# Hybrid decoder layer on one core: two k-steps of the output projection as three fp32r terms

## The chip, the core and the metric

The kernel runs on one core of a Trainium2 chip. A core has TensorE (matmuls into PSUM), VectorE, ScalarE and GpSimd, each of which works through its own instructions in order, and DMA queues, of which this kernel uses that of SyncE (SP) for nearly everything. The engines meet through semaphores. The metric is the time of one execution on the device in microseconds (us). Lower is better. Three runs of the kernel before gave a median of 588.15 us (587.84 to 588.36).

## What is computed

One decoder layer on 256 tokens of width 1024, in fp32. The part that the change touches:

```python
def hybrid_mixer(x, mem, ...):
    h = rms_norm(x, norm_mix_g)
    q_sb, k_sb, v_sb, x_rg, gate_rg, q_ca = jnp.split(h @ w_in, IN_SPLITS, axis=-1)
    o_sb = merge_heads(stick_breaking_attention(...))                 # 512 columns
    hr = rg_lru(causal_depthwise_conv(x_rg, conv_w, conv_b), ...)
    o_rg = gelu(gate_rg) * hr                                         # 256 columns
    o_ca = memory_cross_attention(...)                                # 256 columns
    y = concatenate([rms_norm(o_sb, g_out_sb), rms_norm(o_rg, g_out_rg), rms_norm(o_ca, g_out_ca)])
    return y @ w_out

x = x + hybrid_mixer(...)
x = x + moe_ffn(rms_norm(x, norm_ffn_g), ...)    # 64 experts, 8 for each token, and a shared one
```

## The kernel before

**Stages.** The input projection and the three head groups take the first 84 us. Then comes the output projection, mixed with the end of cross-attention, up to 123 us. Then the router picks the experts and VectorE writes their order to `ids` (at about 137 us). The rest is the experts: TensorE gathers each group's tokens, multiplies, and scatters. The expert weights (3 MB each) stream through cells of 8 KB for each partition, in an order fixed in the code. Six experts are fixed and need no router; their loads and the shared expert's go out before the router is done. A load into a cell waits until TensorE is done with what the cell held.

**Output projection.** y has eight k-steps of 128 columns. Steps 0 to 3 are attention (group 0), 4 and 5 recurrent (group 1), 6 and 7 cross-attention (group 2). Each group is normalised with its own root, so its product is kept apart: `project(u)` (L1612) makes the product of one group, one tile of 128 tokens and one half of 512 columns in PSUM, and VectorE's `residual(u)` (L1153) multiplies it by the group's 1/rms and adds it to x1. There are twelve: the four of group 0, then group 1 and group 2 for tile 0, then for tile 1 in the order group 1, group 2 for each half. The fifth and sixth are thus recurrent, and so are the ninth and the eleventh. A matmul in fp32 leaves two records in the trace, one in fp32r leaves one.

**The sums.** The mean of squares of a group goes ScalarE (`square_and_gain`, L775: the square into `y_sq`, then the gain into `yT`), GpSimd (adds the k-steps, L678 to L684), TensorE (a sum over the partitions, units 26, 33 and 34, L1547), VectorE (`mean_square`, L1148), ScalarE (a root, L850), VectorE (the reciprocal in `residual`). Unit 34 is cross-attention's, and stands in TensorE's program behind the sixth projection and ahead of the seventh.

**What sets the order.** All of it is written out by hand: each engine's program is a list, up to unit 21 by `walk` (L368), after it by the calls in the text. VectorE's program around the change is: gelu's argument, four maxima of cross-attention (`ca_max`), norms, the recurrent scan, the recurrent rows (`yT`, L1188), `ca_evac` 2 and 3 (L1142), `ca_result(0)`, residuals 0 to 2, `ca_result(1)`, residual 3, `mean_square(1)`, residual 4, `mean_square(2)`, residuals 5 to 7, the mean of x1's squares for tile 0, residual 8 and so on. After residual 9 comes `low_part(0)` (L1226) and then residual 10.

**Three terms.** Elsewhere the kernel makes fp32 products from fp32r ones: ScalarE rounds a to a_hi, VectorE makes a_lo = a - a_hi, and TensorE adds a_hi*b_hi + a_lo*b_hi + a_hi*b_lo (L1487, L1509, L1520).

## Time and profile before

| | before |
|---|---|
| median of 3 runs | 588.15 us |
| profiled execution | 588.95 us |
| its span, first to last instruction | 587.2 us |
| TensorE busy | 552.8 us (94%) |
| VectorE busy | 208.9 us (36%) |
| ScalarE busy | 159.2 us (27%) |
| GpSimd busy | 24.3 us (4%) |
| read from HBM | 225.9 MB, 386 GB/s over the span |
| granted clock of TensorE, mean | 0.982 |
| output projection (L1624) on TensorE | 64 records, 29.4 us busy |

The profiled execution is one execution. Its own time is 1.75 us above its span and 0.8 us above the median. Busy times are of an engine's own instructions; a wait shows as idle time ahead of an instruction, with the instruction that ended it. Records of one engine overlap a little, so the distance between starts tells what an instruction costs in a row of its like.

### The profile page before, as it was taken

To read this page: it belongs to the slowest core of one execution; us is meant where nothing else is said; L and a number is where in the kernel's file an instruction comes from. 1 tells how busy PE (TensorE), PEld (TensorE's weight loads), DVE (VectorE), ACT (ScalarE), POOL (GpSimd) and SP (SyncE) were. 2 spreads that over 40 slices of the span, in tenths; PEclk is the share of its full clock that TensorE was granted. 3 is DMA by queue.
4 is the path that set the end of the run, shared out by engine and by line. 5 is a ranking of instruction groups with operands and counts; after the bars stand their busy time and mean duration, and the time that the engine had idled before them with its cause. 6 is when DMAs were issued, how large, how long until landed. Compare 5 with 4: busy or idle time off the path is not lost.

```text
span 587.2 us, 8291 instructions
## 1 busy us (share of the span) xinstructions
PE 552.8 (94%) x3148; PEld 305.7 (52%) x3149; DVE 208.9 (36%) x532; ACT 159.2 (27%) x307; POOL 24.3 (4%) x78
## 2 busy tenths in 40 slices
PE   8999999999999999999999999999969999289994
PEld 6988875465544445555344554555534455034441
DVE  2879789664335222220122222222221222102212
ACT  5786376242212112220021222222221211101112
POOL 1005240000000000000000000000000000000000
PEclk9999999999999999999999999999998999679999
DMA  8997559659999999999999999999999999999993
GB/s 318 418 419 289 214 204 424 253 222 350 424 395 419 423 421 420 427 427 423 426 423 426 426 419 430 431 423 423 424 429 426 431 420 436 428 411 410 417 408 142
DMA packets 26776, 227.50 MB, mean 387 GB/s; under 512 B 3184, under 2 KB 3312, under 8 KB 7664
## 3 DMA queue, kind: packets, MB, share of 16 engines
q1 hardware_dynamic: 26592, 226.93, 93.2%
q8 instruction: 26, 0.43, 0.3%
q14 instruction: 14, 0.11, 0.0%
q10 hardware_dynamic: 144, 0.03, 0.0%
HBM read 225.90 MB, written 1.05 MB: 386 GB/s over the span
## 4 chain that ended last, share of the span: by engine, by line
PE 79%; DMA 14%; DVE 4%; issue 1%; ACT 1%; SPq 0%; DVEq 0%; ACTq 0%
PE ps L1760 30%; PE ps L1789 13%; DMA cell_three<-in_w_e 9%; PE ps L1719 8%; PE ps L1799 7%; DMA cell_two<-in_w_e 5%; PE ps L1624 5%; PE ps L1520 4%; PE ps L1487 3%; PE ps L1501 2%; PE ps L1780 1%; PE ps L1509 1%; DMA wA<-in_w_qk 1%; PE ps L1766 1%; PE ps L1772 1%
## 5 line engine op out<-in xcount | busy, mean ns | idle before, releaser
L1760 PE MATMUL ps<-cell_two,xg 128*64 128x512 f32 (+2 forms) x496 | 110.0, 612 | 18.6 <-DMA cell_three<-in_w_e 14.0
L1789 PE MATMUL ps<-cell_d,e_hT 128*64 128x512 f32 (+2 forms) x440 | 87.6, 597 | 2.2 <-DVE e_hT L1383 1.5
L1760 PE MATMUL ps<-cell_gu,xg 128*64 128x512 f32 (+2 forms) x416 | 78.3, 594 | 0.0
L1380 DVE TENSOR_TENSOR e_h<-e_sg,ps 128x256 f32<-128x256 f32 x28 | 11.8, 421 | 186.2 <-ACT e_sg L897 186.2
L1760 PEld LDWEIGHTS ps<-cell_two,xg 128*64 128x64 f32 (+2 forms) x496 | 34.5, 132 | 82.6 <-issue 82.6
L897 ACT ACTIVATE e_sg<-ps 128x256 f32<-128x256 f32 x28 | 10.8, 384 | 208.5 <-PE ps L1760 208.5
L1438 DVE SCALAR_TENSOR_TENSOR ylo<-ps,gslot,yhi 128x512 fp32r<-128x512 f32 x52 | 39.0, 750 | 72.0 <-ACT yhi L908 72.0
L1719 PE MATMUL ps<-pick,xhi 128*128 128x256 f32 x224 | 58.5, 300 | 0.3 <-DVE pick L1296 0.3
L908 ACT ACTIVATE yhi<-ps,gslot 128x512 fp32r<-128x512 f32 x52 | 35.7, 687 | 69.4 <-PE ps L1789 69.3
L1719 PE MATMUL ps<-pick,xlo 128*128 128x256 f32 x224 | 54.3, 281 | 0.0
L1719 PEld LDWEIGHTS ps<-pick,xhi 128*128 128x128 f32 x224 | 42.2, 188 | 19.1 <-issue 18.8
L1760 PEld LDWEIGHTS ps<-cell_gu,xg 128*64 128x64 f32 (+2 forms) x416 | 25.6, 128 | 47.9 <-issue 47.6
L1789 PEld LDWEIGHTS ps<-cell_d,e_hT 128*64 128x64 f32 (+2 forms) x440 | 25.7, 126 | 40.0 <-issue 39.5
L1799 PE MATMUL ps<-yhi,S 128*128 128x512 f32 x104 | 43.0, 413 | 0.9 <-DVE ylo L1438 0.9
L1719 PEld LDWEIGHTS ps<-pick,xlo 128*128 128x128 f32 x224 | 42.4, 189 | 1.0 <-issue 1.0
L1799 PE MATMUL ps<-ylo,S 128*128 128x512 f32 x104 | 40.9, 393 | 0.0
L1760 PE MATMUL ps<-cell_three,xg 128*64 128x512 f32 (+1 forms) x144 | 37.9, 653 | 0.4 <-DMA cell_three<-in_w_e 0.4
L884 ACT ACTIVATE xg<-ps,vec 128x256 f32<-128x256 f32 x60 | 25.2, 472 | 23.7 <-PE ps L1719 23.6
L1624 PE MATMUL ps<-wo,yT 128*128 128x512 f32 x64 | 29.4, 601 | 0.4 <-DVE x L1163 0.4
L1422 DVE TENSOR_TENSOR xg<-ps,vec 128x512 f32<-128x512 f32 x26 | 18.0, 691 | 30.9 <-PE ps L1719 30.9
L904 ACT CAST S<-ps 128x256 fp32r<-128x256 f32 x26 | 9.7, 372 | 59.7 <-PE ps L1774 59.7
L1377 DVE TENSOR_REDUCE gslot<-ps 64x1 f32<-64x2 f32 (+2 forms) x64 | 10.0, 157 | 42.6 <-ACT S L904 41.4
(336 smaller groups left out, 674.7 us busy)
## 6 DMA issues: line engine op xcount, KB each, us to landing
cell_two<-in_w_e SPq DMA_DIRECT2D x31, 2048.0 KB, 25.8
cell_d<-in_w_e SPq DMA_DIRECT2D x51, 1024.0 KB, 22.1
cell_gu<-in_w_e SPq DMA_DIRECT2D x48, 1024.0 KB, 15.0
cell_three<-in_w_e SPq DMA_DIRECT2D x9, 3072.0 KB, 23.0
wo<-in_w_out SPq DMA_DIRECT2D x1, 4096.0 KB, 12.3
wA<-in_w_qk SPq DMA_DIRECT2D x7, 512.0 KB, 10.8
wR<-in_w_rest SPq DMA_DIRECT2D x3, 1024.0 KB, 28.6
wV<-in_w_v SPq DMA_DIRECT2D x1, 2048.0 KB, 18.8
```

The lines of the kernel that those rows point to most:

```text
L884: nc.scalar.mul(rows_of(c, slice(k, k + 1), slice(0, 2)).squeeze(1), ps[:, Y[step % 2], k % 2 * 2 * P:(k % 2 + 1) * 2 * P].rearrange("p (g ...
L908: nc.scalar.mul(yhi[:, half * 512:(half + 1) * 512], ps[:, Y[half], :], gslot[:, g.routed % 2:g.routed % 2 + 1]).then_inc(yhi_act, 1)
L1380: nc.vector.tensor_tensor(dst[:].rearrange("q k p -> q (k p)"), e_sg[:], ps[:, U, DE:2 * DE], ALU.mult).then_inc(sem, 1)
L1422: nc.vector.tensor_tensor(rows_of(g.chunk + 1, slice(2 * step, 2 * step + 2), slice(0, 2)), ps[:, Y[1], :].rearrange("p (k g s) -> p k g s ...
L1438: nc.vector.scalar_tensor_tensor(ylo[:, c], ps[:, Y[half], :], gslot[:, g.routed % 2:g.routed % 2 + 1], yhi[:, c].bitcast(F32), ALU.mult, ...
L1487: last = mm(b[:, 0:SEQ], part[:, k, :], a[:, k, :], start=k == 0 and m == 0, stop=k == KD - 1 and m == 2)
L1520: last = mm(b, a[:, k, c:c + P], w[:, k, :], start=k == 0 and m == 0, stop=k == KD - 1 and m == 2)
L1624: last = mm(ps[:, ACC[2 * t + half], :], yT[:, k, t * P:(t + 1) * P], wo[:, k, half * 512:(half + 1) * 512], start=k == chunks[0], stop=k ...
L1719: last = mm(o, part[:, t, k, :], pick[c % 2][:, t, :], start=i == 0, stop=i == 3)
L1760: last = mm(ps[side * w:(side + 1) * w, U, :], rows(k, slice(side * w, (side + 1) * w)), weight[:, k - k0, :], start=k == 0, stop=k == KD - 1)
L1789: last = mm(ps[side * w:(side + 1) * w, Y[half], :], e_hT[:, kk, side * w:(side + 1) * w], n[:, kk, half * 512:(half + 1) * 512], start=kk ...
L1799: last = mm(ps[:, ACC[2 * t + half], :], to_token[:, t * P:(t + 1) * P], y[:, half * 512:(half + 1) * 512], start=False, stop=sem is not N ...
```

## The change

w_out's k-steps 4 and 5 and the recurrent rows get high and low parts in fp32r. ScalarE makes `wo_hi` in `walk` (two casts of 128x1024, `split_o`), and the gained high rows `y_hi` (the two gains first, then the two squares; the gain is no longer written to `yT`). VectorE makes `wo_lo` ahead of its first maximum (`weight_low`) and `y_lo` behind `ca_evac(2)` and `ca_evac(3)` (`gain_low`). TensorE's fp32 products of steps 4 and 5 become three fp32r ones each. The parts lie where cells lie: `wo_hi` in that of low 5, so this load now waits until the eleventh projection is done, `wo_lo` in w_out's own place. `x1_sq` moves, so that down 6 need not wait for it. The loads around it are in another order.

```diff
--- before.py
+++ after.py
@@ -183,6 +183,10 @@
     wA = [at(f"wA{n}", o_A + 4 * KB * n, [P, KD, P]) for n in range(8)]
     wA_lo = [at(f"wA_lo{n}", o_A + 4 * KB * n, [P, KD, P], F32R) for n in range(8)]
     wo = at("wo", o_A, [P, KD, D])
+    wo_hi = at("wo_hi", o_ring + 80 * KB, [P, 2, D], F32R)
+    wo_lo = at("wo_lo", o_A + 16 * KB, [P, 2, D], F32R)
+    y_hi = at("y_hi", o_O + 16 * KB + 64, [P, 2, SEQ], F32R)
+    y_lo = at("y_lo", o_O + 12 * KB, [P, 2, SEQ], F32R)
     res = at("res", o_A, [P, NT, D])
     xg = at("xg", o_A, [P, KD // 2, 2, 2, P])
 
@@ -202,7 +206,7 @@
     rg_t = r("rg_t", [P, 2, SEQ])
     rg_u = r("rg_u", [P, 2, SEQ])
     y_sq = at("y_sq", o_R + 16 * KB, [P, KD, SEQ])
-    x1_sq = at("x1_sq", o_R + 8 * KB, [P, D])
+    x1_sq = at("x1_sq", o_A, [P, D])
     xhi = at("xhi", o_R, [P, NT, KD, P], F32R)
     xn2T = at("xn2T", o_R + 16 * KB, [P, KD, SEQ])
     yhi = at("yhi", o_R + 16 * KB, [P, D], F32R)
@@ -370,7 +374,7 @@
             if 3 <= i <= 10:
                 walk.append(("t", i - 3))
             walk += {1: [("split_w", 2)], 2: [("split_w", 3)], 3: [("split_u", 14)], 4: [("split_u", 15), ("split_u", 16)],
-                     5: [("split_u", 17)], 6: [("ca_square", 0)], 7: [("conv", 0)], 8: [("ca_norm", 0)], 9: [("conv", 1)],
+                     5: [("split_u", 17)], 6: [("ca_square", 0)], 7: [("conv", 0)], 8: [("ca_norm", 0)], 9: [("split_o", 0), ("split_o", 1), ("conv", 1)],
                      12: [("gelu", 0)]}.get(i, [])
 
 
@@ -536,16 +540,18 @@
             load_fixed("high", 4)
             load_fixed("down", 3)
             load_fixed("down", 4)
-            load_fixed("low", 5)
             load_fixed("low", 6)
+            sp.wait_ge(wo_ps, 4)
+            load_shared("low")
+            sp.wait_ge(yrg_dve, 2)
+            load_fixed("down", 6)
             sp.wait_ge(unit_ps, 33)
             load_fixed("high", 5)
+            sp.wait_ge(wo_ps, projections.index((1, 1, 1)) + 1)
+            load_fixed("high", 6)
+            load_fixed("low", 5)
             sp.wait_ge(wo_ps, len(projections))
-            load_fixed("high", 6)
             load_fixed("down", 5)
-            load_shared("low")
-            sp.wait_ge(ssq_act, 7)
-            load_fixed("down", 6)
             sp.wait_ge(rt_ps, NT)
             load_fixed("down", 2)
 
@@ -809,6 +815,9 @@
                 elif kind == "ca_norm":
                     act.wait_ge(ca_ss_dve, 1)
                     nc.scalar.activation(ca_rs[:], ca_rs[:], ACT.Sqrt).then_inc(ca_rt_act, 1)
+                elif kind == "split_o":
+                    act.wait_ge(wo_loaded, 16)
+                    nc.scalar.copy(wo_hi[:, n, :], wo[:, 4 + n, :]).then_inc(whi_act, 1)
                 elif kind == "gelu":
 
                     act.wait_ge(unit_ps, 18)
@@ -845,7 +854,12 @@
                 if g:
                     for i in range(2):
                         act.wait_ge(yrg_dve if g == 1 else oca_dve, i + 1)
-                        square_and_gain(2 + 2 * g + i)
+                        if g == 1:
+                            nc.scalar.mul(y_hi[:, i, :], yT[:, 4 + i, :], vec[:, GOUT + 4 + i:GOUT + 5 + i]).then_inc(yg_act, 1)
+                        else:
+                            square_and_gain(6 + i)
+                    for i in range(2 if g == 1 else 0):
+                        nc.scalar.activation(y_sq[:, 4 + i, :], yT[:, 4 + i, :], ACT.Square).then_inc(ysq_act, 1)
                 freed(act, SUMS[g])
                 nc.scalar.activation(g_rs[:, g, :], g_rs[:, g, :], ACT.Sqrt).then_inc(g_rt_act, 1)
 
@@ -1113,6 +1127,8 @@
                     link(nc.vector.reduce_sum(ca_rs[:].rearrange("p a t h -> p (a t h)"),
                                               ca_sq[:].rearrange("p a t (h d) -> p (a t h) d", d=HD), AX.X))
                     nc.vector.tensor_scalar(ca_rs[:], ca_rs[:], 1.0 / HD, EPS, ALU.mult, ALU.add).then_inc(ca_ss_dve, 1)
+                elif kind == "split_o":
+                    continue
                 elif kind == "ca_norm":
                     dve.wait_ge(ca_rt_act, 1)
                     link(nc.vector.reciprocal(ca_rs[:], ca_rs[:]))
@@ -1163,6 +1179,17 @@
                 nc.vector.scalar_tensor_tensor(x1[:, t, c], ps[:, ACC[2 * t + half], :], g_rs[:, g, t:t + 1], x1[:, t, c],
                                                ALU.mult, ALU.add).then_inc(x1_dve, 1)
 
+            def weight_low(i):
+                dve.wait_ge(whi_act, len(splits) + i + 1)
+                nc.vector.tensor_tensor(wo_lo[:, i, :], wo[:, 4 + i, :], wo_hi[:, i, :].bitcast(F32), ALU.subtract).then_inc(wlo_dve, 1)
+
+            def gain_low(i):
+                dve.wait_ge(yg_act, 5 + i)
+                nc.vector.scalar_tensor_tensor(y_lo[:, i, :], yT[:, 4 + i, :], vec[:, GOUT + 4 + i:GOUT + 5 + i],
+                                               y_hi[:, i, :].bitcast(F32), ALU.mult, ALU.subtract).then_inc(alo_dve, 1)
+
+            weight_low(0)
+            weight_low(1)
             for h in range(CA_HEADS):
                 ca_max(h)
 
@@ -1187,7 +1214,9 @@
             for c in range(2):
                 nc.vector.tensor_tensor(yT[:, 4 + c, :], rg_g[:, c, :], rg_r[:, c, :], ALU.mult).then_inc(yrg_dve, 1)
             ca_evac(2)
+            gain_low(0)
             ca_evac(3)
+            gain_low(1)
             ca_result(0)
             dve.wait_ge(x1_loaded, 16)
             for u in range(3):
@@ -1618,11 +1647,18 @@
 
                     pe.wait_ge(x1_dve, projections.index((g - 1, t, half)) + 1)
                 chunks = ((0, 1, 2, 3), (4, 5), (6, 7))[g]
+                o, c = ps[:, ACC[2 * t + half], :], slice(half * 512, (half + 1) * 512)
                 for k in part or chunks:
                     if t == 0 and half == 0:
                         pe.wait_ge(yg_act, k + 1)
-                    last = mm(ps[:, ACC[2 * t + half], :], yT[:, k, t * P:(t + 1) * P],
-                              wo[:, k, half * 512:(half + 1) * 512], start=k == chunks[0], stop=k == chunks[-1])
+                    if g != 1:
+                        last = mm(o, yT[:, k, t * P:(t + 1) * P], wo[:, k, c], start=k == chunks[0], stop=k == chunks[-1])
+                        continue
+                    if t == 0 and half == 0:
+                        pe.wait_ge(wlo_dve, len(splits) + k - 3)
+                        pe.wait_ge(alo_dve, 1 + KD + k - 3)
+                    for m, (y, w) in enumerate(((y_hi, wo_hi), (y_lo, wo_hi), (y_hi, wo_lo))):
+                        last = mm(o, y[:, k - 4, t * P:(t + 1) * P], w[:, k - 4, c], start=k == 4 and m == 0, stop=k == 5 and m == 2)
                 if k == chunks[-1]:
                     last.then_inc(wo_ps, 1)
```

TensorE's program between the sums of the recurrent group (unit 33) and of cross-attention (unit 34), before:

```order
L1547 MATMUL ps<-ones,y_sq 128x1 [waits ysum_pool,unit_dve]
L1547 MATMUL ps<-ones,y_sq 128x1
L1624 MATMUL ps<-wo,yT 128x512 [waits yg_act,x1_dve]
L1624 MATMUL ps<-wo,yT 128x512 [waits yg_act]
L1624 MATMUL ps<-wo,yT 128x512 [waits x1_dve]
L1624 MATMUL ps<-wo,yT 128x512
L1547 MATMUL ps<-ones,y_sq 128x1 [waits ysum_pool,unit_dve]
```

and after:

```order
L1576 MATMUL ps<-ones,y_sq 128x1 [waits ysum_pool,unit_dve]
L1576 MATMUL ps<-ones,y_sq 128x1
L1661 MATMUL ps<-wo_hi,y_hi 128x512 [waits wlo_dve,alo_dve,yg_act,x1_dve]
L1661 MATMUL ps<-wo_hi,y_lo 128x512
L1661 MATMUL ps<-wo_lo,y_hi 128x512
L1661 MATMUL ps<-wo_hi,y_hi 128x512 [waits alo_dve,wlo_dve,yg_act]
L1661 MATMUL ps<-wo_hi,y_lo 128x512
L1661 MATMUL ps<-wo_lo,y_hi 128x512
L1661 MATMUL ps<-wo_hi,y_hi 128x512 [waits x1_dve]
...
L1576 MATMUL ps<-ones,y_sq 128x1 [waits ysum_pool,unit_dve]
```

Four fp32 products became twelve fp32r ones; the sum behind them has kept its place and its waits.

VectorE's program from gelu's argument to the first maximum, before:

```order
L1065 TENSOR_TENSOR rg_g<-gate 128x512 [waits unit_dve]
L1066 TENSOR_SCALAR rg_g<-rg_g 128x512 [waits dve_chain]
L1067 TENSOR_TENSOR rg_g<-rg_g,gate 128x512 [waits dve_chain]
L1125 TENSOR_REDUCE mx<-ps 128x2 [waits unit_ps]
L1126 TENSOR_SCALAR mx<-mx 128x2 [waits dve_chain]
```

and after, with the stretch from the copies of cross-attention's weights (`ca_evac(2)`) to the mean of the recurrent group behind it:

```order
L1079 TENSOR_TENSOR rg_g<-gate 128x512 [waits unit_dve]
L1080 TENSOR_SCALAR rg_g<-rg_g 128x512 [waits dve_chain]
L1081 TENSOR_TENSOR rg_g<-rg_g,gate 128x512 [waits dve_chain]
L1184 TENSOR_TENSOR wo_lo<-wo,wo_hi 128x1024 [waits whi_act] x2
L1141 TENSOR_REDUCE mx<-ps 128x2 [waits unit_ps]
...
L1158 COPY ca_pT_201<-ps 128x512 [waits oca_ps,unit_ps]
L1188 SCALAR_TENSOR_TENSOR y_lo<-yT,vec,y_hi 128x256 [waits yg_act]
L1158 COPY ca_pT_202<-ps 128x512 [waits unit_ps]
L1188 SCALAR_TENSOR_TENSOR y_lo<-yT,vec,y_hi 128x256 [waits yg_act]
L1162 COPY yT<-ps 128x256 [waits unit_ps]
```

Two subtractions stand ahead of the maxima, and a low part behind each of the two copies.

The SP queue from down 4 to down 2, before. The cells: 59 is low 5, 60 low 6, 67 high 5, 61 high 6, 122 down 5, 69 shared low, 123 down 6, 131 down 2.

```order
L459 DMA cell_d_118<-in_w_e 128x2048
L459 DMA cell_gu_59<-in_w_e 128x2048
L459 DMA cell_gu_60<-in_w_e 128x2048
L459 DMA cell_gu_67<-in_w_e 128x2048 [waits unit_ps]
L459 DMA cell_gu_61<-in_w_e 128x2048 [waits wo_ps]
L459 DMA cell_d_122<-in_w_e 128x2048
L459 DMA cell_gu_69<-in_w_gu_sh 128x2048
L459 DMA cell_d_123<-in_w_e 128x2048 [waits ssq_act]
L459 DMA cell_d_131<-in_w_e 128x2048 [waits rt_ps]
```

and after:

```order
L463 DMA cell_d_118<-in_w_e 128x2048
L463 DMA cell_gu_60<-in_w_e 128x2048
L463 DMA cell_gu_69<-in_w_gu_sh 128x2048 [waits wo_ps]
L463 DMA cell_d_123<-in_w_e 128x2048 [waits yrg_dve]
L463 DMA cell_gu_67<-in_w_e 128x2048 [waits unit_ps]
L463 DMA cell_gu_61<-in_w_e 128x2048 [waits wo_ps]
L463 DMA cell_gu_59<-in_w_e 128x2048
L463 DMA cell_d_122<-in_w_e 128x2048 [waits wo_ps]
L463 DMA cell_d_131<-in_w_e 128x2048 [waits rt_ps]
```

Low 5 has moved back by five places, shared low and down 6 have moved ahead of high 5.

## Rows read from the trace of the kernel before

**Rows 1.** The page's DMA line: busy tenths in 40 slices of 14.7 us.

```profile
DMA  8997559659999999999999999999999999999993
```

**Rows 2.** TensorE's waits: what, for whom, us in total, times, longest.

```profile
PE ps L1760 <- DMA cell_three<-in_w_e: 14.4, 2, 14.0
```

**Rows 3.** The SP queue's waits, the same columns.

```profile
SPq L557 <- DVE ids L1318: 9.4, 1, 9.4
```

**Rows 4.** The chain of waits: start us, us, what.

```profile
59.32 5.47 PE ps L1520 x24
...
115.28 0.76 DVE x L1163
```

**Rows 5.** Timeline of TensorE: start, us, line, form, count, [idle before].

```profile
105.57 3.68 PE L1624 MATMUL ps<-wo,yT 128*128 128x512 f32 x8
109.09 0.50 PE L1547 MATMUL ps<-ones,y_sq 128*128 128x1 f32 x4
...
120.90 1.88 PE L1624 MATMUL ps<-wo,yT 128*128 128x512 f32 x4
```

**Rows 6.** Timeline of GpSimd: its sums of squares.

```profile
86.83 1.27 POOL L678 TENSOR_TENSOR y_sq<-y_sq 128x512 f32<-128x512 f32 x1 [3.84 <-ACT y_sq L777]
...
102.53 0.72 POOL L684 TENSOR_TENSOR y_sq<-y_sq 128x256 f32<-128x256 f32 x1 [13.62 <-ACT y_sq L777]
107.74 0.73 POOL L684 TENSOR_TENSOR y_sq<-y_sq 128x256 f32<-128x256 f32 x1 [4.48 <-ACT y_sq L777]
```

**Rows 7.** Timeline of ScalarE.

```profile
80.68 0.48 ACT L808 COPY wT<-ps 128x384 f32<-128x384 f32 x1 [2.71 <-PE ps L1583]
...
101.59 0.49 ACT L778 ACTIVATE yT<-yT,vec 128x256 f32<-128x256 f32 x1
...
107.26 0.40 ACT L777 ACTIVATE y_sq<-yT 128x256 f32<-128x256 f32 x1
```

**Rows 8.** Timeline of VectorE.

```profile
85.48 0.69 DVE L1067 TENSOR_TENSOR rg_g<-rg_g,gate 128x512 f32<-128x512 f32 x1
88.50 0.69 DVE L1125 TENSOR_REDUCE mx<-ps 128x2 f32<-128x512 f32 x1 [2.33 <-PE ps L1541]
...
101.48 1.28 DVE L1142 COPY ca_pT<-ps 128x512 f32<-128x512 f32 x2
...
106.26 0.15 DVE L1150 TENSOR_SCALAR g_rs<-ps 128x2 f32<-128x2 f32 x1
...
119.97 0.75 DVE L1163 SCALAR_TENSOR_TENSOR x<-ps,g_rs,x 128x512 f32<-128x512 f32 x1
```

**Rows 9.** ScalarE's casts by line: duration ns min/median/max, first and last start.

```profile
L768 ACT CAST hi_unit<-wR x4: 1068/1071/1072, 49.7 to 60.5; 128x1024 fp32r<-128x1024 f32 x4
```

**Rows 10.** The load of w_out by tile: issue at 64.8 us, and time to landing.

```profile
L523 SPq DMA_DIRECT2D wo<-in_w_out x1: 328/328/328, 64.8 to 64.8; - x1
...
DMA to landing us min/median/max: 12.3/12.3/12.3
```

**Rows 11.** Windows: us, busy of PE, PEld, DVE, ACT, POOL, granted clock, DMA, GB/s.

```profile
88.50:106.40 17.90, 17.90 (x76) 9.46 (x74) 17.38 (x42) 9.78 (x26) 1.14 (x2) 1.00 1.01 424
```

**Rows 12.** Timeline of VectorE, earlier: instructions with two operands from SBUF.

```profile
45.64 0.51 DVE L1095 TENSOR_TENSOR beta<-beta,rest 128x256 f32<-128x256 f32 x1
...
46.07 2.37 DVE L1031 TENSOR_TENSOR w_kv_lo<-w_kv,w_kv_hi 128x2048 fp32r<-128x2048 f32 x1
...
57.82 0.42 DVE L1095 TENSOR_TENSOR beta<-beta,rest 128x256 f32<-128x256 f32 x1
58.15 2.35 DVE L1038 TENSOR_TENSOR wR_lo<-wR,hi_unit 128x1024 fp32r<-128x1024 f32 x2
```

**Rows 13.** Timeline of GpSimd over the same stretch: selects that read SBUF.

```profile
46.26 2.59 POOL L651 TENSOR_SCALAR_AFFINE_SELECT beta<-beta 128x128 f32<-128x128 f32 x2
...
60.92 0.54 POOL L651 TENSOR_SCALAR_AFFINE_SELECT beta<-beta 128x128 f32<-128x128 f32 x2
```

**Rows 14.** VectorE's low parts of the memory rows, by line, columns as in rows 9.

```profile
L1021 DVE SCALAR_TENSOR_TENSOR memT_lo<-memT_in,vec,memT_hi x8: 479/479/480, 39.1 to 41.9; 128x256 fp32r<-128x256 f32 x8
```

## The prediction

> **What bounds the kernel now.** I read the views in this order: the page's DMA line, the waits of TensorE and of the SP queue, the chain of waits, then the engines' timelines from 84 to 124 us.
>
> From the tenth of the forty slices on, from 132 us, the DMA engines are busy to nine tenths or more until the last slice [rows 1]. Late in the kernel TensorE waits 14.4 us for expert weights [rows 2]. So the stream of expert weights sets the end, and what counts is when it starts. Its first load needs the experts' numbers from VectorE, and the SP queue waits 9.4 us for them with nothing else to issue [rows 3]. The output projection lies ahead of that. If it ends D later, the numbers come D later, and so do the groups that free the cells: the kernel ends D later, and in the same way earlier. The question is how far the last projection product moves.
>
> Two facts decide that. First, the chain of waits runs through VectorE's residual add at 115.28 us [rows 4]. This add stands in VectorE's program behind a mean that needs ScalarE's square; TensorE's ninth projection is done before it. Second, TensorE's row sum for cross-attention (unit 34) starts at 109.09, directly behind the recurrent projections that start at 105.57 [rows 5]. It needs GpSimd's sum, done at 107.74 + 0.73 = 108.47 [rows 6]. That needs ScalarE's square of 107.26 [rows 7], which is queued on ScalarE behind a root that waits for VectorE's mean of 106.26 [rows 8]. With 0.08 us for the signal (my estimate) unit 34 could start at 108.55. So the path from VectorE has **0.54 us of slack** there and no more.
>
> **The products.** Four fp32 products are the 8 records from 105.57 to 109.09: 3.52 / 4 = 0.88 us each [rows 5]. In the kernel's own fp32r work, with the same high, low, high pattern, 24 matmuls of 512 columns take 5.47 us, 0.228 each, so three take 0.69 [rows 4]. Each of the eight replaced products saves 0.19 us, 1.5 in all. Of that, on the path:
> - Four (0.76 us) stand before unit 34. TensorE is done at 108.3 in place of 109.09, but unit 34 needs GpSimd until 108.55 even if VectorE loses nothing. The gain here is at most 0.54, and each 0.1 that VectorE is later takes 0.1 of it.
> - Two stand in the ninth projection. What follows waits for the add of 115.28 in any case: nothing.
> - Two stand in the eleventh. The twelfth starts at 120.90 and needs the residual that VectorE does from 119.97 for 0.75, so until 120.72 [rows 5, 8]. VectorE comes to that add from its low part, not from TensorE. Of the 0.38 saved, **0.14** arrive (120.90 less 120.76).
>
> **ScalarE's added work.** Two casts of 128x1024 at 1.07 each [rows 9] go ahead of a copy before which ScalarE is idle for 2.71 us, up to 80.68 [rows 7]. 2.1 fits, if w_out is there at 78: it is issued at 64.8 and lands 12.3 later, at 77.1 [rows 10]. I cost them at nothing. If they were late, the copy and TensorE behind it would be late by the excess. Of the recurrent rows the two gains now come ahead of the two squares; a gain takes 0.49 and a square 0.40 [rows 7], so the squares end some 0.4 later. The recurrent sum was done at 102.53 + 0.72 [rows 6] and is read just before 105.57, so this is covered.
>
> **VectorE's added work.** VectorE is busy for 17.38 of the 17.90 us from 88.50 to 106.40 [rows 11]; the rest are short waits within its own chains. So what delays it here delays the mean of 106.26 in full.
> - The two subtractions of 128x1024 stand ahead of the first maximum. A pair takes 2.35 [rows 12], and would run from 86.10, behind the product of 85.48, to 88.45. The maximum started at 88.50 after 2.33 of idle time [rows 8]. Alone they cost nothing.
> - But GpSimd's first sum of squares starts at 86.83 and takes 1.27 [rows 6], until now in VectorE's idle time. The trace shows that such instructions exclude each other: two GpSimd selects took 2.59 us while VectorE ran a subtraction from 46.07 for 2.37, against 0.54 at 60.92 [rows 12, 13]. VectorE loses too: its product at 45.64, with selects around it, took 0.51, against 0.42 at 57.82 [rows 12]. There GpSimd, waiting behind one VectorE instruction, got in ahead of the next one. So here GpSimd waits from 86.83 until the first subtraction is done at 87.24, gets in, and the second subtraction waits. For how long: sums of 512 and 256 columns take 1.27 and 0.73, so 256 columns read for 0.54 and 512 for 1.08. Bounds are 0 (VectorE keeps its turn and GpSimd is late instead, with room to spare) and 1.27. I take 1.08, the value nearest to the rows, less some 0.1 of cover: **+0.95**. A gain is excluded, as work is only added.
> - The two low parts of the gained rows. Eight like them start from 39.1 to 41.9, so 0.40 apart, at 0.48 each [rows 14]: **+0.8**, at most 0.96.
> - The second low part would start at 101.48 + 0.6 (copy) + 0.4 + 0.6 = 103.08 [rows 8]. GpSimd's recurrent sum, at 102.53 before, comes 0.4 later by ScalarE's new order, at 102.93, and reads for 0.54. The same conflict again: **+0.45**. Bounds are 0, if VectorE comes first, and 0.57.
>
> The Trainium skill speaks against this change: "SBUF — State Buffer", section "SBUF: two separate sides", says that a VectorE instruction with two SBUF inputs and a GpSimd instruction that reads SBUF share an exclusive port, and that whichever starts first keeps it to its end while the other is blocked. The rows at 46.26 and 45.64 agree. By the rule the time is the sum below; without it, that of the rival "no conflict".
>
> **The sum.** VectorE's mean comes 0.95 + 0.8 + 0.45 = 2.2 us later. 0.54 of it is slack, so unit 34 starts 1.66 later, and TensorE's residual products behind it as well. The last projection takes back 0.14. That makes **+1.5 us**. The profiled execution took 588.95 (a span of 587.2 and 1.75 around it), 0.8 above the median of the three runs, 588.15. Against its own time the sum gives 590.45, against the median **589.7 us**.
>
> **The weight loads.** In both orders all loads of fixed experts are issued before the queue begins its 9.4 us wait for the experts' numbers [rows 3]. Shared low and down 6 go out earlier, low 5 later, high 6 one projection earlier. That wait covers what they gain or lose, so I cost them at nothing. If loads were still queued when the numbers came, 1 MB less of them would be worth up to 3.1 us (w_out's 4 MB in 12.3 [rows 10]).
>
> **Rivals.**
> - *One conflict only.* If GpSimd gets in only at the weights, +1.1, 589.2; if only at the rows, +0.6, 588.7. For it speaks that 0.15 us decide at the rows. Chance 0.25.
> - *No conflict.* VectorE is 0.8 later, unit 34 by 0.26, less 0.14: 588.3. Chance 0.13.
> - *The products' gain arrives.* If what follows each product waited for TensorE alone, all 1.5 would count: 586.7. Against it stand the slack of 0.54 and the add of 115.28. Chance 0.09.
> - *The clock falls.* TensorE would idle for about 2 us before unit 34. The granted clock was 1.00 (2.4 GHz) in this stretch [rows 11]. If it fell to 1.2 GHz, the six products behind it (5.2 us at 0.88) could take up to twice as long: up to 594.9. It decides from the length of the gap, and no gap as long lies in these rows. Chance 0.06.
> - *The casts are late.* If w_out landed 1 us later than at 78, 590.7. Chance 0.04.
> - *The change doesn't do what it says.* If the fp32r products cost as much as before, TensorE would be done at 109.09, still before unit 34's new start; only the 0.14 would go. No case of its own.
>
> **How the numbers follow.** The forecast has 0.43, its own range is 589.2 to 590.2. A measurement of this kernel can tell about 0.2% from no change: below 586.97 or above 589.33. Faster is the gain that arrives, 0.09. Slower is most of the forecast, 0.36, a third of "only at the weights", 0.05, the clock and the casts: 0.50 with rounding. Same is the rest, 0.41. The range takes in "no conflict" with its spread and the upper bounds of the conflicts: 587.9 to 590.5. Outside are the full gain, most of the clock, and half of the casts.
>
> **What would show it.** GpSimd's first sum starts near 86.83 and takes some 1.7 us in place of 1.27. The second subtraction takes about 2.3 in place of 1.2, and the first maximum starts at 89.5. The mean of 106.26 comes at 108.5, and unit 34 at 110.8 behind a wait for GpSimd. The fp32r products take 0.23 each. The last projection starts at 122.4, and the experts' numbers come 1.5 us later. I am wrong if the second subtraction takes 1.2, if unit 34 follows the projections directly, or if the numbers and the end don't move by the same amount.

## The result: 0.4% slower, about one microsecond more than forecast

The changed kernel's first comparison gave a median of 591.25 us (589.79 to 592.37, 8 executions) against 588.16: a ratio of **1.0043** [1.0031, 1.0054] (95% interval in brackets, here and below), +2.5 us by the ratio and +3.1 by the medians where +1.5 was forecast, and outside the range that ended at 590.5. Four repeats gave 1.0040 [1.0027, 1.0053], 1.0053 [1.0037, 1.0069], 1.0041 [1.0028, 1.0054] and 1.0035 [1.0019, 1.0052]. One slow execution of before (941.75 us, mean granted clock 0.558) is left out of everything below.

The direction was right, and so was the forecast of how late the experts' numbers come. What the forecast left out is that TensorE's clock falls in some executions behind the wait that the change makes; the section after this one and the experiments lead there. From here on, "after" is the changed kernel. The profiled execution took 589.79 us (span 588.0, mean granted clock 0.982). Executions differ a little in where they stand on the time axis, so the start of VectorE's product for gelu is the common mark, and the difference between the marks of two executions (the offset) is taken off. Here is VectorE's timeline (start, us, line, form, count) with this product and the numbers, first before, then after:

```profile
84.30 0.68 DVE L1065 TENSOR_TENSOR rg_g<-gate 128x512 f32<-128x512 f32 x1
...
135.87 0.21 DVE L1318 CAST ids<-ps 1x58 int32<-1x58 f32 x1
```

```profile
84.46 0.68 DVE L1079 TENSOR_TENSOR rg_g<-gate 128x512 f32<-128x512 f32 x1
...
86.25 3.43 DVE L1184 TENSOR_TENSOR wo_lo<-wo,wo_hi 128x1024 fp32r<-128x1024 f32 x2
89.60 0.68 DVE L1141 TENSOR_REDUCE mx<-ps 128x2 f32<-128x512 f32 x1
...
103.17 0.47 DVE L1188 SCALAR_TENSOR_TENSOR y_lo<-yT,vec,y_hi 128x256 fp32r<-128x256 f32 x1
...
104.17 0.86 DVE L1188 SCALAR_TENSOR_TENSOR y_lo<-yT,vec,y_hi 128x256 fp32r<-128x256 f32 x1
...
108.44 0.15 DVE L1166 TENSOR_SCALAR g_rs<-ps 128x2 f32<-128x2 f32 x1
...
137.61 0.21 DVE L1347 CAST ids<-ps 1x58 int32<-1x58 f32 x1
```

The offset is 0.16, and the numbers come 137.61 - 135.87 - 0.16 = **1.58 us later**. The two subtractions take 3.43 as a pair where such a pair took 2.35 [rows 12], the second low part 0.86 beside 0.47 for the first, and the mean is 108.44 - 0.16 - 106.26 = 2.0 late [rows 8]. GpSimd's timeline of after answers to [rows 6]:

```profile
86.99 1.61 POOL L684 TENSOR_TENSOR y_sq<-y_sq 128x512 f32<-128x512 f32 x1 [3.84 <-ACT y_sq L783]
88.67 1.59 POOL L685 TENSOR_TENSOR y_sq<-y_sq 128x256 f32<-128x256 f32 x1
104.02 0.73 POOL L690 TENSOR_TENSOR y_sq<-y_sq 128x256 f32<-128x256 f32 x1 [13.75 <-ACT y_sq L862]
109.92 0.73 POOL L690 TENSOR_TENSOR y_sq<-y_sq 128x256 f32<-128x256 f32 x1 [5.17 <-ACT y_sq L783]
```

The first sum takes 1.61 in place of 1.27, and the pair of subtractions beside it 3.43 in place of 2.35. I read this as the sum waiting for the first subtraction and then holding up the second. The last sum starts 2.0 late, and TensorE's timeline (answering to [rows 5]) shows what waits for it:

```profile
106.27 0.50 PE L1661 MATMUL ps<-wo_hi,y_hi 128*128 128x512 f32 x1 [0.35 <-DVE x L1179]
...
108.94 0.40 PE L1661 MATMUL ps<-wo_lo,y_hi 128*128 128x512 f32 x1
110.79 0.58 PE L1576 MATMUL ps<-ones,y_sq 128*128 128x1 f32 x4 [1.45 <-POOL y_sq L690]
111.23 3.68 PE L1655 MATMUL ps<-wo,yT 128*128 128x512 f32 x8
...
122.55 1.98 PE L1655 MATMUL ps<-wo,yT 128*128 128x512 f32 x4
```

The last matmul of the sixth projection starts at 108.94. Before, unit 34 followed directly; now it waits 1.45. The fifth projection starts at 106.27, which is 0.54 late net of the offset, since it now waits for VectorE's residual; this hides in the same wait. The last projection starts at 122.55, 1.49 later than at 120.90 net of the offset. ScalarE's casts were hidden, as its timeline shows: the copy that [rows 7] has at 80.68 starts at 80.84, the offset and no more.

```profile
78.02 2.00 ACT L820 CAST wo_hi<-wo 128x1024 fp32r<-128x1024 f32 x2
80.84 0.48 ACT L814 COPY wT<-ps 128x384 f32<-128x384 f32 x1 [0.82 <-PE ps L1612]
```

TensorE still waits for the stream. Its two long waits are 13.0 and 4.3 us, where they were 14.0 [rows 2] and 4.7, and a third one of 0.4 is gone:

```profile
PE ps L1796 <- DMA cell_three<-in_w_e: 13.0, 1, 13.0
PE ps L1796 <- DMA cell_two<-in_w_e: 4.3, 1, 4.3
```

### The profile page after: what moved, and what is told of

Its sections match the earlier page's. It is cut to its first block, busy times and chain, and to the rows that moved or that the text cites. A ratio compares the mean times of both kernels' runs of the same rounds, so it can differ in the third digit from the quotient of the medians.

```text
span 588.0 us, 8315 instructions
## 1 busy us (share of the span) xinstructions
PE 553.6 (94%) x3156; PEld 307.5 (52%) x3157; DVE 213.5 (36%) x536; ACT 161.0 (27%) x309; POOL 25.4 (4%) x78
## 4 chain that ended last, share of the span: by engine, by line
PE 77%; DMA 10%; DVE 8%; issue 2%; ACT 1%; POOL 0%; SPq 0%; POOLq 0%; DVEq 0%; ACTq 0%
PE ps L1796 32%; PE ps L1825 14%; PE ps L1755 9%; PE ps L1835 7%; DMA cell_two<-in_w_e 5%; DMA cell_three<-in_w_e 4%; PE ps L1549 4%; PE ps L1530 2%; PE ps L1516 1%; PE ps L1655 1%; PE ps L1816 1%; PE ps L1538 1%; PE ps L1802 1%; DMA wA<-in_w_qk 1%; PE ps L1808 1%
## 5 line engine op out<-in xcount | busy, mean ns | idle before, releaser
L1655 PE MATMUL ps<-wo,yT 128*128 128x512 f32 x48 | 22.3, 605 | 0.7 <-DVE x L1179 0.7
```

What stands on the lines that cost most here:

```text
L1655: last = mm(o, yT[:, k, t * P:(t + 1) * P], wo[:, k, c], start=k == chunks[0], stop=k == chunks[-1])
```

## Where the last microsecond comes from

The mean granted clock of an execution turned out to sort the times. Median us of the executions at each mean clock, and their number, over the comparisons that follow (for after the first one too). "Late by five" and "late by seven" are the kernel before with five or seven copies put ahead of the routing; the last row is the changed kernel with three repairs of its order. All are described below.

| | 0.983 and over | 0.980 to 0.982 | 0.979 and under |
|---|---|---|---|
| before | 588.23 (25) | 588.68 (51) | none |
| after | none | 590.41 (17) | 592.01 (9) |
| before, late by five | 589.25 (3) | 589.89 (9) | 591.37 (2) |
| before, late by seven | 590.29 (1) | 592.07 (1) | 592.24 (4) |
| waits and orders repaired | 586.14 (5) | 587.15 (6) | none |

In the middle column after is 1.7 above before, close to the 1.58 at the numbers. The rest of its surplus is nine executions of 26 at a lower clock, and none in the first column. The columns were chosen after the fact, and within one the times still spread by up to 1.7 us: the two profiled executions, 588.95 and 589.79, are both at 0.982 and only 0.84 apart. So the table shows where to look and doesn't prove a cause. The experiments follow in the order in which they led there. "Numbers" is always the shift of VectorE's `ids` against before, net of the offset.

## Experiments

**The changed kernel again.**

> The changed kernel once more, unaltered, for another profile. Its eight runs so far lie from 589.8 to 592.4 us. In the traces the experts' numbers come about 1.6 us later than before, as forecast, while the median rose by 3.1. Theory A (clock): the other 1.5 us come from TensorE's clock; an execution above 591.5 shows a mean granted clock near 0.979 in place of 0.982, and its trace shows one more stretch at half clock in which TensorE has work. Theory B (loads): they come from the new order of the weight loads, and the experts' stream lands later than the delay of the numbers explains, at the same clock. Expected by both: median 590 to 592, the numbers at 138.8 us.

Measured: 590.68 us, 1.0040 [1.0027, 1.0053]; numbers +1.58 (at 137.97; the 138.8 expected was too late). The first result holds. The profiled execution is at 0.982, so theory A could not be looked at.

**No overlap of GpSimd and VectorE.** GpSimd starts each sum behind VectorE's instructions with two SBUF operands.

```diff
             pool.wait_ge(ysq_act, 4)
+            pool.wait_ge(wlo_dve, len(splits) + 2)
...
                 pool.wait_ge(ysq_act, k + 2)
+                pool.wait_ge(alo_dve, 1 + KD + 2)
```

> The changed kernel, with GpSimd's first sum of squares waiting until both subtractions of w_out's parts are done, and its later sums waiting until both low parts of the rows are done. If the two engines' shared reading costs what the trace shows (first maximum at 89.6 in place of 88.5, second low part 0.86 in place of 0.47 us), the mean of the recurrent group moves from 108.4 back to about 107.0, unit 34 from 110.8 to about 109.5, and the median falls by 1.3 to 1.4 us against the changed kernel, to some 0.2 us above before in the front, plus what theories A or B leave. If the conflict is not the cause, nothing moves.

Measured: 589.16, **1.0012** [1.0003, 1.0021]; numbers +0.77, so keeping the engines apart is worth 0.81 at the numbers. That is less than expected: the mean is at 107.66 in place of 107.0, and unit 34 at 110.0 in place of 109.5. The timelines of this kernel, GpSimd and VectorE:

```profile
88.78 1.27 POOL L685 TENSOR_TENSOR y_sq<-y_sq 128x512 f32<-128x512 f32 x1 [5.60 <-DVE wo_lo L1186]
...
104.41 0.73 POOL L692 TENSOR_TENSOR y_sq<-y_sq 128x256 f32<-128x256 f32 x1 [13.56 <-DVE y_lo L1190]
```

```profile
86.27 2.35 DVE L1186 TENSOR_TENSOR wo_lo<-wo,wo_hi 128x1024 fp32r<-128x1024 f32 x2
88.67 0.69 DVE L1143 TENSOR_REDUCE mx<-ps 128x2 f32<-128x512 f32 x1
89.39 0.67 DVE L1144 TENSOR_SCALAR mx<-mx 128x2 f32<-128x2 f32 x1
```

Sum and pair are back at 1.27 and 2.35. The small `mx` instruction takes 0.67 where others of its form take 0.17, and ends at 90.06, with GpSimd's sum (88.78 + 1.27 = 90.05). So half a microsecond of the conflict moved to it, and the 0.81 is less than the whole cost of the conflicts.

**The weight loads alone.** Before with after's order of loads on SP.

```diff
-            load_fixed("low", 5)
             load_fixed("low", 6)
+            sp.wait_ge(wo_ps, 4)
+            load_shared("low")
+            sp.wait_ge(yrg_dve, 2)
+            load_fixed("down", 6)
             sp.wait_ge(unit_ps, 33)
             load_fixed("high", 5)
...
```

> The kernel before, with the new order of the weight loads and x1's squares in their new place, and nothing else. Theory A: no change, within 0.1%, since the SP queue waits 9.4 us for the experts' numbers in either order. Theory B: slower by about 1.5 us, with the numbers at the same time and later landings of the experts' weights.

Measured: 588.70, 1.0006 [0.9998, 1.0015]; numbers at 0.0. No cost that can be measured; +1.5 is excluded.

**A delay alone.** Before, with five instructions of VectorE that change nothing, each waited for, ahead of the mean.

```diff
+            for _ in range(5):
+                link(nc.vector.tensor_scalar(rg_i[:], rg_i[:], 1.0, None, ALU.mult))
             mean_square(1, RG)
```

> The kernel before, with five extra VectorE instructions of 128x512 (2.2 us together) ahead of the mean of the recurrent group, nothing else. The mean moves from 106.3 to about 108.5, unit 34 to about 110.8, the experts' numbers by +1.6. Forecast of the rigid shift: median +1.6 us. Theory A: +1.6 to +3.1, with the same spread of clocks as the changed kernel. Theory B: +1.6 and no more.

Measured: 590.74, **1.0048** [1.0036, 1.0061]; numbers +1.87, and TensorE's timeline has the wait ahead of unit 34:

```profile
111.08 0.58 PE L1549 MATMUL ps<-ones,y_sq 128*128 128x1 f32 x4 [1.66 <-POOL y_sq L684]
```

Nothing of the change is in this kernel, and it loses as much. So a delay alone is enough for the surplus; it needs neither the parts, nor the stores, nor the loads.

**Dearer products.** After, with three of four second-group pairs back to one fp32 product of the high parts (the small terms of these pairs are left out).

```diff
+                    if t or half:
+                        last = mm(o, y_hi[:, k - 4, t * P:(t + 1) * P].bitcast(F32), wo_hi[:, k - 4, c].bitcast(F32), start=k == 4, stop=k == 5)
+                        continue
```

> The changed kernel with three of the four pairs of its second-group projections (all but the one of tile 0, first half) back to one fp32 product each, of y_hi and wo_hi (the two small terms of these pairs are left out). TensorE then spends 6 x (0.88 - 0.69) = 1.2 more in that group, all the parts are still made. It asks what the cheaper products are worth. Theory of the prediction (unit 34 is held by VectorE's and GpSimd's chain, the products lie before it): TensorE ends the group by 110.1, unit 34 waits about 0.3 for GpSimd in place of 1.5, and the end moves by 0 to +0.3 against the changed kernel, 590.7 to 591.0 here (ratio to before 1.0040 to 1.0050). Rival (the products are on the path): +1.2, 591.9 (1.0061).

Measured: 590.72, 1.0044 [1.0028, 1.0059]; numbers +1.59, as after. TensorE waits 1.14 ahead of unit 34 in place of 1.45, not the 0.3 expected: only two of the six products stand ahead of unit 34, and what these two save (0.31) goes into that wait. The other four, behind it, are worth 0.12 at the start of the last projection and nothing at the numbers.

**The delay ahead of the routing.** Before, with a clearing and five copies in place (`pad` is a scratch tile) on VectorE.

```diff
             x1_rstd(1)
+            link(nc.vector.memset(pad[:], 0.0))
+            for _ in range(5):
+                link(nc.vector.tensor_scalar(pad[:], pad[:], 1.0, None, ALU.mult))
             route()
```

> The kernel before with one clearing and five copies in place (128x512, each waited for, about 2.2 to 2.6 in all) on VectorE just ahead of the routing, when TensorE has nothing left to do before it; nothing ahead of that place moves. The same delay put before the mean of the recurrent group gave +2.4 at the end for +1.9 at the numbers. Theory A (each microsecond at the numbers comes to more at the end, because of TensorE's clock behind the last waits for the stream): the end moves by the delay plus 0.3 to 0.8, here about 591.0 to 591.4 (ratio 1.0046 to 1.0055), and executions at a mean clock of 0.979 are among the runs. Theory B (the surplus arises in the front, in TensorE's gap before unit 34): the end moves by the delay alone, 590.5 to 590.8 (1.0037 to 1.0042), and the mean clock stays at 0.982 and over.

Measured: 589.85, 1.0024 [1.0013, 1.0035]; numbers +1.56. This looked like theory B, but the interval overlaps that of after.

**A smaller delay.** Two instructions in place of five ahead of the mean.

> The kernel before with two extra operations in place of the five of the earlier run, ahead of the mean of the recurrent group: about 1.0 at the mean, 0.5 to 0.8 at unit 34 and the numbers, since its slack goes first. A rigid end: 588.8 to 589.1 (ratio 1.0008 to 1.0013). An end that moves by 1.25 times the delay: 588.9 to 589.3 (1.0010 to 1.0017). A surplus that comes in one step, once the delay passes some point: as rigid here, since it would not be reached.

Measured: 589.16, 1.0014 [1.0005, 1.0024]; numbers +0.48, TensorE's wait 0.27. The three expectations overlap, so this tells little.

**The waits repaired.** The kernel without overlap; on ScalarE the squares and gains of group 2 stand ahead of the root of group 1.

```diff
+                    for i in range(2 if g == 1 else 0):
+                        act.wait_ge(oca_dve, i + 1)
+                        square_and_gain(6 + i)
                 freed(act, SUMS[g])
                 nc.scalar.activation(g_rs[:, g, :], g_rs[:, g, :], ACT.Sqrt).then_inc(g_rt_act, 1)
```

> The changed kernel with two repairs: GpSimd starts its sums behind VectorE's subtractions (as in the run without overlap), and ScalarE squares and gains the two steps of the third group before it takes the root of the second group's sums, so that unit 34 no longer stands behind the mean on VectorE. Theory: the last sum on GpSimd starts by 106 to 107 in place of 109.1, unit 34 follows the last product of the second group at 108.3 to 109.0 (before: 109.09, with the wait ahead of it), and the numbers come 0 to 0.8 before those of the kernel before: 587.4 to 588.3 (ratio 0.9984 to 1.0000). Rival: the residual additions on VectorE take over as what is late, and it stays where the run without overlap was, 589.2 (1.0012).

Measured: 587.92, **0.9988** [0.9979, 0.9997]; numbers -0.58. TensorE's timeline shows unit 34 directly behind the sixth projection:

```profile
108.27 0.40 PE L1664 MATMUL ps<-wo_lo,y_hi 128*128 128x512 f32 x1
108.50 0.50 PE L1579 MATMUL ps<-ones,y_sq 128*128 128x1 f32 x4
```

With that wait gone the loss is gone, although all of the change is still there. Net of the offset unit 34 is at 108.44, 0.65 earlier than before, and it follows the products directly, so here their gain can arrive.

**The changed kernel for its profile, and ten instructions ahead of the mean in place of five.**

> The changed kernel once more, for its profile: executions of it are at a mean clock of 0.982 (589.8 to 590.9) or of 0.979 (591.6 to 592.4), and both profiles so far are of the first kind. If the profiled one is of the second, theory F (the clock falls in TensorE's gap ahead of unit 34) shows a stretch of reduced granted clock between 105 and 120 with the numbers later by another 0.5 to 1.5; theory T (the surplus lies behind the waits for the stream) shows the front as before and a longer or a third stretch of reduced clock behind 400.

Measured: 592.15, 1.0053 [1.0037, 1.0069]; numbers +1.57. The profiled execution was at 0.982 again and decided nothing.

> The kernel before with ten extra operations (128x512, each waited for) ahead of the mean of the recurrent group in place of five: 4.9 at the mean, about 4.2 at unit 34 and at the numbers, and TensorE idle for about 4 ahead of unit 34 in place of 1.7. Theory F (that gap lowers the clock): the numbers come up to 1 to 3 later than by the delay, the granted clock falls between 105 and 120, the end at +5.5 to +8 (ratio 1.009 to 1.014). Theory T (1.5 times at the end for whatever delay beyond 1.5): +6.3 (1.0107) with a full clock in the front. A rigid end: +4.2 (1.0071). A surplus that is a fixed sum: +5.1 (1.0087).

Measured: 595.29, **1.0112** [1.0096, 1.0127]; numbers +7.3 in the profiled execution (596.68, the slowest of the four), far more than the delay of 4.1 at unit 34. TensorE's timeline of this kernel, and its windows (stretch, length, busy, granted clock, DMA share, GB/s):

```profile
113.46 0.99 PE L1549 MATMUL ps<-ones,y_sq 128*128 128x1 f32 x4 [3.97 <-POOL y_sq L684]
114.31 8.14 PE L1626 MATMUL ps<-wo,yT 128*128 128x512 f32 x12
```

```profile
108.00:111.00 3.00, 1.49 (x4) 1.00 0.99 410
111.00:115.00 4.00, 1.54 (x5) 0.75 0.16 68
115.00:125.00 10.00, 9.64 (x23) 0.76 0.00 0
```

Behind the wait of 3.97 the granted clock falls from 1.00 to 0.75 in the mean of these stretches: part of the time TensorE runs at 1.2 GHz in place of 2.4. Twelve records take 8.14; in the timeline of before the same twelve take 5.40:

```profile
109.45 5.40 PE L1624 MATMUL ps<-wo,yT 128*128 128x512 f32 x12
```

All four executions were at 0.977 to 0.979.

**A later start of the stream with the front untouched.** Seven copies ahead of the routing in place of five.

> The kernel before with one clearing and seven copies in place ahead of the routing in place of five: the numbers 2.5 later (five gave 1.56 net of the execution's own offset, and the end +1.4). Theory T (the surplus hangs on how late the numbers are): past 1.6 the end moves by 1.3 to 1.6 times the delay, 3.2 to 4.0 (ratio 1.0055 to 1.0068), with executions at 0.979. Theory F (it hangs on the gap in the front): the end moves by the delay, +2.3 to +2.6 (1.0039 to 1.0044), none at 0.979.

Measured: 592.10, 1.0060 [1.0044, 1.0075]; numbers +2.47 in the profile, which is at 0.984; the three others are at 0.979. I read this as theory T. The last profiles show otherwise.

**VectorE's order as well.** The repaired kernel, with residual 8 ahead of the mean of x1 and `low_part(0)` ahead of the routing.

```diff
-            x1_mean(0)
             residual(8)
+            x1_mean(0)
...
-            low_part(0)
             residual(10)
...
             x1_rstd(1)
+            low_part(0)
             route()
```

> The kernel with the repaired waits and ScalarE's order, and VectorE's order changed behind it: the ninth addition ahead of the mean of x1's tile 0 (which waits 1.3 for ScalarE), and the low part of tile 0 (1.28) from ahead of the eleventh addition to the 1.3 of idle time ahead of the routing. Theory: TensorE's last projections come 0.7 to 1.3 earlier, the numbers and the end by as much: 586.6 to 587.3 (ratio 0.9966 to 0.9980; without these moves it was 0.9988). Rival (the squares of tile 1 on ScalarE set the routing): no gain, 0.9988.

Measured: 586.65, **0.9966** [0.9954, 0.9978]; numbers -1.58. TensorE's wait for VectorE's x1 ahead of the tenth projection is gone.

**Front or late, on one chip.** After, the delay of five ahead of the routing, and the last kernel again, side by side.

> The changed kernel, beside the late delay on one chip. Numbers +1.6, as in all its profiles. Theory P (place: the surplus comes with TensorE's gap of 1.1 to 1.7 ahead of unit 34): ratio 1.0040 to 1.0050, at least 0.0015 above the late delay. Theory N (only the lateness of the numbers counts; the late delay's 1.0024 was a low draw): 1.0035 to 1.0045 and the late delay within 0.0010 of it.

Measured: 590.41, 1.0041 [1.0028, 1.0054]; numbers +1.56.

> The kernel before with one clearing and five copies ahead of the routing, as in the first late delay: numbers +1.56, the front untouched. Theory P: ratio 1.0020 to 1.0030. Theory N: 1.0033 to 1.0045.

Measured: 590.25, 1.0033 [1.0021, 1.0045]; numbers +1.54. Within 0.0010 of after, as theory N says, though both intervals reach into the range of theory P. Two of its executions were at 0.979, with the front untouched. So a gap ahead of unit 34 isn't needed for that clock; whether it lies behind 400 or at a third place was open.

> The version with the repaired waits and the orders of ScalarE and VectorE changed, once more on this chip: its numbers 1.6 before those of the kernel before, ratio 0.9966 [0.9954, 0.9978] on the other chip. A rigid end gives 0.9973 (-1.6), an end that moves by 1.3 to 1.6 times as much 0.9958 to 0.9965.

Measured: 586.14, **0.9959** [0.9946, 0.9972]; numbers -1.60. Over both comparisons this version is 1.5 us faster than before in executions at 0.980 to 0.982 (587.15 against 588.68), close to its 1.6 at the numbers, and 2.1 faster in those at 0.983 and over (586.14 against 588.23). Three of the five executions here are of the second kind, so the ratio itself lies nearer to the second expectation than to the rigid end.

**The place of the lower clock.**

> The changed kernel, for a profile of an execution at 0.979. Theory T: the reduced stretches behind the waits for the stream (from 440 and from 508) are together some 3 longer than in the profiles at 0.982, and nothing else differs. Theory 3 (a third place): a reduced stretch where none of the profiles has one, in the front or near 472.

Measured: 590.66, 1.0035 [1.0019, 1.0052]. The profiled execution, 591.64, is at 0.979, and its rows show the place. TensorE's timeline and windows:

```profile
110.69 0.58 PE L1576 MATMUL ps<-ones,y_sq 128*128 128x1 f32 x4 [1.45 <-POOL y_sq L690]
111.13 5.38 PE L1655 MATMUL ps<-wo,yT 128*128 128x512 f32 x8
```

```profile
108.00:111.00 3.00, 1.55 (x9) 1.00 0.99 410
111.00:115.00 4.00, 4.00 (x8) 0.57 0.77 324
115.00:125.00 10.00, 9.29 (x42) 1.00 0.13 28
```

The wait of 1.45 is the same as in the first profile of after, and there the next stretch is at full clock:

```profile
108.00:111.00 3.00, 1.55 (x8) 1.00 0.98 410
111.00:115.00 4.00, 4.00 (x14) 1.00 0.84 348
```

With the lower clock the same eight records take 5.38 in place of 3.68, **+1.70**, and the numbers come at 139.19 in place of 137.61 (1.67 later net of the offset). The waits for the stream, 12.8 and 4.1, are as in the first profile of after (13.0 and 4.3), and the stretches of lower clock behind them as well: 0.86 from 430 to 455 and 0.77 from 500 to 530 in both. So theory T is out. The medians of after at 0.979 and at 0.982 differ by 592.01 - 590.41 = 1.60. It is the same program; in some executions the clock falls there and in others not. This is one profile: that the other eight executions at 0.979 have their lower clock in the same place is inferred from their time and mean clock.

> One clearing and seven copies ahead of the routing, as before (1.0060, three executions of four at 0.979). The same two theories for its profile; the front up to 125 as in the kernel before.

Measured: 592.30, 1.0066 [1.0042, 1.0090]; profile at 0.979, 592.53. TensorE's timeline and window:

```profile
133.76 0.20 PE L1701 MATMUL ps<-picked,upper 128*128 128x64 bf16 x1 [2.39 <-DVE picked L1259]
```

```profile
136.00:140.00 4.00, 4.00 (x22) 0.57 0.28 117
```

A late delay makes a gap as well, while TensorE waits for the routing (2.39 here, none before). The clock falls behind it, in the gathers, and the numbers come 3.6 late in place of 2.5. The earlier profile of the same kernel, at 0.984, has the same wait of 2.39 and a granted clock of 1.00 in this window. So the late delays' surplus is of the same kind as that of after, and needs nothing behind 400.

> One clearing and eleven copies: the numbers 4.3 later. A rigid end at equal clock: 592.8 at 0.982 (ratio 1.0073 to 1.0078), 594.4 at 0.979. If the level falls further with the delay: 0.979 or below in all executions, 594 to 595.5 (1.0098 to 1.012).

Measured: 594.59, 1.0101 [1.0081, 1.0121]; two of three executions at 0.976. The wait for the routing is 4.2, the numbers are 6.3 late where 4.3 was expected. The granted clock is 0.80 from 133 to 136 and 0.50 from 136 to 140.

## Point by point

- **Right: the stream sets the end.** At like clock the end moved as the numbers did: +1.7 for +1.58 (after), -1.5 for -1.6 (both orders repaired). In the middle column the other kernels agree within 0.45: +0.8 for +0.77 (no overlap), +0.3 for 0.0 (loads alone), +1.7 for +1.87 (delay alone), +2.0 for +1.59 (dearer products), +1.2 for +1.55 (late by five), +0.5 for +0.48 (smaller delay), -0.6 for -0.58 (waits repaired).
- **Right: the slack of 0.54 and the products' gain.** The mean was 2.0 late (2.2 forecast), unit 34 1.54 (1.66), the last projection 1.49 (1.5). With six of eight products back in fp32, the numbers did not move. The fp32r products run 0.23 apart. Two small steps were off and cost nothing: TensorE was not done at 108.3 but at about 109.0 net of the offset, since the fifth projection started 0.54 late behind VectorE's residual, and the 0.14 of the eleventh projection came to 0.05 at the last projection and to nothing at the numbers.
- **Right: the conflict at the weights.** The first maximum came 0.94 late net of the offset (0.95 forecast). At the rows it took 0.39 (0.45). By the Trainium skill, "SBUF — State Buffer", section "SBUF: two separate sides", the engine that starts first holds the shared port to its end while the other is blocked. The trace agrees: 1.61 for GpSimd's sum and 3.43 for VectorE's pair, 1.27 and 2.35 when kept apart. That the waiting GpSimd gets in between two subtractions that stand back to back is a reading of the same rows; no run tests it by itself.
- **Right: casts and weight loads at nothing** (80.84; 1.0006).
- **Wrong: the rival "the clock falls".** It was called a case of its own, with a chance of 0.06, at up to 594.9, and left outside the range. It isn't one outcome among others but something that happens in part of the executions of the same program, 9 of 26, at +1.6 each. So it belonged in the sum as a share (9/26 of 1.6 is 0.55 in the mean), and its price is not a doubling of all six products: the reduced clock ended within the eight records behind unit 34, and cost 1.70. Nor are six fp32 products behind unit 34 after the change: the last two of them are the ninth projection, now three fp32r terms each. The sentence "no gap as long lies in these rows" was true, and it was a reason for a wide range, not for a small chance. The gap itself was 1.45, not "about 2", since the fifth projection was late. This is the step that failed: the sum charged the gap only with its delay, and put the clock behind it at nothing.
- **Wrong: "the kernel ends D later".** For D as a number at the end, the sum also needed a term for the clock behind the waits for the stream. A third of before's executions (25 of 76) are at 0.983 or over, none of the 26 of after. That is worth up to 0.45, the distance of before's two columns. The profiles show where the clock differs (granted clock, mean of the stretch):

| profiles | mean clock | 430 to 455 us | 500 to 530 us |
|---|---|---|---|
| loads alone, delay alone, late by five (second), late by seven (first) | 0.984 | 0.93 | 0.77 |
| before, waits repaired, one of the five of after (the second repeat) | 0.982 | 0.93 | 0.72 |
| the four others of after, no overlap, dearer products, smaller delay, late by five (first), late by seven (second), the two with both orders repaired | 0.979 to 0.982 | 0.86 | 0.77 |

So against an execution at 0.984 the ones at 0.982 have more of the lower clock in one of the two stretches, and it differs in which; the one at 0.979 has the stretch from 111 to 115 on top. The profile of before and the first of after lie in different rows of the table and in the same column of times. What tips it stays open. It isn't lateness alone: both profiles of the version with both orders repaired are in the last row, with numbers 1.6 early, and three with late numbers are in the first.
- **The account.** Over all executions the median went from 588.44 to 590.77, +2.33. Of this 1.73 is the distance in the middle column, forecast as 1.5; 0.24 is that before's median lies below its own middle column, by the executions in its first column, of which after has none; 0.36 is that the nine executions at 0.979 lift the median of after above 590.41. In the first comparison they were four of eight, and its 591.25 stands between the two groups: how far the first measurement lay outside the range is in part the luck of the draw.

## To carry to other kernels

Where a sum waits for another engine, cheaper matmuls ahead of it only lengthen the wait: follow the chain backwards first (here TensorE, GpSimd, ScalarE, VectorE), and move what it doesn't need behind it. The same change is 0.3 to 0.4% faster than before once GpSimd keeps off VectorE's two-operand instructions, ScalarE does the squares ahead of an unrelated root, and VectorE puts its additions first. No run has these orders without the fp32r products, so what the products add to this is not shown; my estimate for unit 34 in the kernel with the waits repaired is 0.65, since its twelve fp32r matmuls take 2.87 from start to start (105.63 to 108.50) and the eight records before 3.52. And a new gap on TensorE ought to be priced with the clock behind it: look at the granted clock of every execution, not of the profiled one alone.

## What was unexpected of the hardware

- The clock may fall behind short waits, and not each time. In this kernel: of TensorE's waits ahead of unit 34, those of 3.97 went with a mean clock of 0.979 and under in 4 of 4 executions, 1.66 in 2 of 6, 1.45 in 9 of 26, 1.23 in 0 of 11, 1.14 in 0 of 4. Of its waits for the routing, those of 4.24 did in 2 of 3, 2.39 in 4 of 6, 1.47 in 2 of 14. The waits are of the profiled executions. These are counts of this kernel, too few for a rule.
- An instruction of VectorE with a single SBUF tensor operand of 2 columns (the `mx` one in the kernel without overlap) took 0.67 in place of 0.17 beside GpSimd's sum, and ended with it.
- GpSimd's second sum of 256 columns took 1.59 in after, where before it took 0.73 (at 88.19). It started at 88.67, while VectorE was in the second subtraction, which fits the same conflict.
